# Rope of the up-projected queries: exchanging the halves by transfers in place of a second product

## The reference, cut to what matters

```python
def _rope(x, cos, sin):
    half = x.shape[-1] // 2
    x1, x2 = x[..., :half], x[..., half:]
    return jnp.concatenate([x1 * c - x2 * s, x2 * c + x1 * s], axis=-1)

def _mla(cq, ckv, kr, g_q, w_q_up, g_kv, w_kv_up, cos, sin):
    q = (_rms(cq, g_q) @ w_q_up).reshape(B, L, MLA_HEADS, MLA_NOPE + MLA_ROPE)   # 4 heads of 128 + 64, rank 256
    q_nope = q[..., :MLA_NOPE]
    q_rope = _rope(q[..., MLA_NOPE:], cos[:, None, :], sin[:, None, :])
```

## Time and profile before

| what | value |
|---|---|
| median of 3 runs | 2604.51 us |
| profiled execution, its own time | 2604.58 us |
| its span, first to last instruction | 2602.8 us |
| mean granted TensorE clock | 0.998 |
| TensorE (PE) busy | 2547.2 us, 98% |
| VectorE (DVE) busy | 1616.4 us, 62% |
| ScalarE (ACT) busy | 1213.5 us, 47% |
| GpSimd (POOL) busy | 334.6 us, 13% |

### The profile page before, as it was taken

One profiled execution on the slowest core, in us unless ns is written; L12 is line 12 of the kernel. 1 busy time (PEld: TensorE's weight loads), 2 busy tenths in 40 slices (PEclk: granted clock), 3 DMA queues, 4 the chain that ended last, 5 costly groups with the idle time before them and its releaser, 6 DMA issues.

```text
span 2602.8 us, 35370 instructions
## 1 busy us (share of the span) xinstructions
PE 2547.2 (98%) x12220; PEld 2106.9 (81%) x12220; DVE 1616.4 (62%) x3499; ACT 1213.5 (47%) x2183; POOL 334.6 (13%) x366
## 2 busy tenths in 40 slices
PE   8999999999999999999999999999999999999998
PEld 7998888676667888877877888888888888888886
DVE  6123306998995676664458677776757465564665
ACT  6112314777765555554545333533335353443554
POOL 2110002222221222210000000000000001111143
PEclk9999999999999999999999999999999999999999
DMA  6334458553332111135677767757655365666787
GB/s 232 121 106 125 126 163 253 143 135 85 95 131 90 35 32 38 36 111 162 195 244 217 227 197 237 222 177 222 192 155 181 107 225 110 168 168 159 202 165 138
DMA packets 329436, 398.59 MB, mean 153 GB/s; under 512 B 21408, under 2 KB 235664, under 8 KB 320944
## 3 DMA queue, kind: packets, MB, share of 16 engines
q1 hardware_dynamic: 311696, 364.41, 44.6%
q0 software_dynamic: 17568, 31.99, 8.0%
HBM read 239.86 MB, written 156.48 MB: 152 GB/s over the span
## 4 chain that ended last, share of the span: by engine, by line
PE 62%; DVE 3%; DMA 2%; ACT 1%; issue 1%; SPq 0%; POOL 0%; DVEq 0%; ACTq 0%; POOLq 0%
PE ff_ps_x L3248 26%; PE ff_ps_m L3248 13%; PE ff_ps_z L3248 6%; PE ml_ps_s L2125 6%; PE ff_ps_m L1685 4%; PE ml_ps_o L2154 4%; PE ml_ps_t L2138 2%; DMA ml_v_raw<-scr_yT 1%; DMA ff_pieces<-scr_acc 0%; PE ff_ps_r L2685 0%; PE mo_ps_t L2702 0%; SPq L2312 0%; DVE ff_pieces L2415 0%; DVE ff_pieces L2606 0%; DVE ff_pieces L2602 0%
## 5 line engine op out<-in xcount | busy, mean ns | idle before, releaser
L3248 PE MATMUL ff_ps_x<-ff_mv_hi_p,ff_st_hi_p 128*128 128x512 f32 x764 | 297.8, 390 | 0.5 <-ACT ff_u L2988 0.5
L3248 PE MATMUL ff_ps_x<-ff_mv_lo_p,ff_st_hi_p 128*128 128x512 f32 x764 | 297.3, 389 | 0.0
L3248 PE MATMUL ff_ps_x<-ff_mv_hi_p,ff_st_lo_p 128*128 128x512 f32 x764 | 297.3, 389 | 0.0
L2125 PE MATMUL ml_ps_s<-wide,ml_qs 128*128 128x416 f32 (+14 forms) x880 | 195.2, 354 | 4.0 <-PEq L137 2.7
L3094 DVE TENSOR_TENSOR ff_st_lo_p<-ff_ps_m,ff_st_hi_p 128x512 fp32r<-128x512 f32 x190 | 130.7, 688 | 103.4 <-ACT ff_st_hi_p L2971 103.4
L2938 POOL DMA_DIRECT2D scr_acc<-ff_pieces x64 | 55.6, 874 | 1015.2 <-DVE ff_pieces L3118 946.7
L2988 ACT ACTIVATE ff_u<-ff_ps_x 128x512 f32<-128x512 f32 x128 | 76.6, 598 | 215.0 <-PE ff_ps_x L3248 215.0
L3248 PEld LDWEIGHTS ff_ps_x<-ff_mv_hi_p,ff_st_hi_p 128*128 128x128 f32 x764 | 143.4, 188 | 32.5 <-issue 2.0
L3248 PEld LDWEIGHTS ff_ps_x<-ff_mv_hi_p,ff_st_lo_p 128*128 128x128 f32 x764 | 143.4, 188 | 29.9
L3248 PEld LDWEIGHTS ff_ps_x<-ff_mv_lo_p,ff_st_hi_p 128*128 128x128 f32 x764 | 143.4, 188 | 29.6
L2125 PEld LDWEIGHTS ml_ps_s<-wide,ml_qs 128*128 128x128 f32 x880 | 149.5, 188 | 20.0 <-issue 7.0
(11 more groups left out here) (316 smaller groups left out, 6380.4 us busy)
## 6 DMA issues: line engine op xcount, KB each, us to landing
st_raw<-in_w_ff SPq DMA_DIRECT2D x64, 512.0 KB, 6.2
scr_hid<-ff_pieces SPq DMA_DIRECT2D x128, 256.0 KB, 2.7
st_raw<-scr_hid SPq DMA_DIRECT2D x64, 512.0 KB, 5.4
ring<-in_w_ff SPq DMA_DIRECT2D x28, 1024.0 KB, 7.6
scr_t<-ring SPq DMA_DIRECT2D x24, 1024.0 KB, 5.8
ring<-scr_t SPq DMA_DIRECT2D x21, 1024.0 KB, 7.6
scr_acc<-ff_pieces POOLq DMA_DIRECT2D x64, 256.0 KB, 3.8
ring<-scr_u SPq DMA_DIRECT2D x13, 1024.0 KB, 8.2
```

The lines of the kernel that those rows point to most:

```text
L2125: m = pe.matmul(ps_s[n % NSB][:, 0:w], q, k, start=j == 0, stop=j == len(pairs) - 1)
L3248: m = pe.matmul(bank[:, :], w[kind][:, k], a[kind][:, k], start=start and k == 0 and i == 0, stop=stop and k == KH - 1 and i == 2, skip_gr ...
```

## The change: what it does

- A rope job makes one product (6 matmuls) in one bank. ACT copies it to one of four places (`rots`). SP exchanges the halves of each head by four transfers of 32 partitions, within SBUF (`swap`). VectorE multiplies the copy and the exchanged copy by cosines and sines in place (`finish`), POOL adds, SP stores.
- `FINISH_AT` says after which job the ropes of each piece are finished: those of piece 0 after rope (1, 1), of piece 1 after rope (2, 1), of piece 2 after rope (3, 1), of piece 3 after the last q job.
- The q jobs go behind the last rope. Takers of q and vo jobs are now ACT, ACT, VectorE in turn.
- The rope weights are split in the value pass, before ACT's last copy and after VectorE's last low part there; the exchanged weights and their four loads are gone.
- `UP_OUTS` is 6. The wait for all rope sums moves from the first transposes of the first head to its group 2.

```diff
@@ cv_proj, scalar
             for n in range(N):
                 m, rows = N + n, TILES[n][1]
+                if n == N - 1:
+                    act.wait_ge(up.gained, QR // P)
+                    act.activation(up.rope_hi[:, :, :], up.q_raw[:, :, NQF:WQ], ACT.Copy).then_inc(up.rope_hi_ready, 1)
@@ cv_proj, vector
             low(N - 1, pt[(N - 1) % 2])
+            dve.wait_ge(up.rope_hi_ready, 1)
+            dve.tensor_tensor(up.rope_lo[:, :, :], up.q_raw[:, :, NQF:WQ], f32(up.rope_hi[:, :, :]), ALU.subtract).then_inc(up.rope_lo_ready, 1)
@@
-WQ = NQF + 2 * NR
-UP_Q_LOADS = 4 * (QR // P) + 1
+WQ = NQF + NR
+UP_Q_LOADS = 2 * (QR // P) + 1
@@ mla_up, the jobs
-        jobs += [("q", 0, h) for h in range(MLA_H)] + [("turn", TURN_V)] + ropes_of(2) + folds_of((0, 1)) + ropes_of(3) + folds_of((2, 3))
-        WO_AT = {jobs.index(("rope", piece, 0)): piece - 2 for piece in (2, 3)}
+        jobs += [("turn", TURN_V)] + ropes_of(2) + folds_of((0, 1)) + ropes_of(3) + [("q", 0, h) for h in range(MLA_H)] + folds_of((2, 3))
+        WO_AT = {jobs.index(("turn", TURN_V)): 0, jobs.index(("rope", 3, 0)): 1}
+        FINISH_AT = {jobs.index(job): (2 * piece, 2 * piece + 1)
+                     for piece, job in enumerate((("rope", 1, 1), ("rope", 2, 1), ("rope", 3, 1), ("q", 0, MLA_H - 1)))}
@@
-            takers.append({"rope": "dve", "turn": "dve", "fold": "dve"}.get(kind) or ("act", "dve")[copies % 2])
+            takers.append({"rope": "act", "turn": "dve", "fold": "dve"}.get(kind) or ("act", "act", "dve")[copies % 3])
@@ sync
+            def swap(r):
+                sp.wait_ge(taken["act"], taken_by[ropes[r]])
+                raw, changed = (rots[r % ROTS][:, j] for j in range(2))
+                for p0 in range(0, P, ROPE):
+                    for to, of in ((0, ROPE // 2), (ROPE // 2, 0)):
+                        sp.dma_start(changed[p0 + to:p0 + to + ROPE // 2], raw[p0 + of:p0 + of + ROPE // 2]).then_inc(swapped[r % ROTS], 16)
+            for i, (kind, *args) in enumerate(jobs):
+                if kind == "rope":
+                    if args == [2, 0]:
+                        load_first_rest(sp, io, scr, ahead, 1)
+                    if args == [3, 0]:
+                        load_first_head(sp, io, scr, ahead, 2)
+                    swap(ropes.index(i))
+                elif i in stores:
+                    store(i)
+                for r in FINISH_AT.get(i, ()):
+                    store(ropes[r])
@@ gpsimd
-                pool.wait_ge(taken["dve"], taken_by[i])
+                pool.wait_ge(finished, r + 1)
@@ scalar
+                elif kind == "rope":
+                    r = ropes.index(i)
+                    if r >= ROTS:
+                        act.wait_ge(added, r - ROTS + 1)
+                    act.wait_ge(sums_ready, i + 1)
+                    act.activation(rots[r % ROTS][:, 0], at(i)[:, :], ACT.Copy).then_inc(taken["act"], 1)
@@ vector
+            def finish(r):
+                piece = jobs[ropes[r]][1]
+                dve.wait_ge(trig_loaded[piece], 16)
+                dve.wait_ge(swapped[r % ROTS], 64 * (r // ROTS + 1))
+                for part in range(2):
+                    m = dve.tensor_tensor(rots[r % ROTS][:, part], rots[r % ROTS][:, part], trig[:, part, cols(piece)], ALU.mult)
+                m.then_inc(finished, 1)
@@ vector, after each job
+                for r in FINISH_AT.get(i, ()):
+                    finish(r)
@@
-UP_OUTS = 8
+UP_OUTS = 6
```

More of the change, by code:

```diff
@@ L857, in mla_up @@
             first_banks.append(bank)
-            bank += 2 if kind == "rope" else 1
+            bank += 1
         ahead.up_taken = [(taken[who], takers[:-LAST].count(who)) for who in taken]
@@ L861, in mla_up @@
         ahead.ropes_added = added
-        stores = [i for i, job in enumerate(jobs) if job[0] in ("q", "vo", "rope")]
         ropes = [i for i, job in enumerate(jobs) if job[0] == "rope"]
+        stores = []
+        for i, job in enumerate(jobs):
+            stores += [i] * (job[0] in ("q", "vo")) + [ropes[r] for r in FINISH_AT.get(i, ())]
+        outs = {i: n for n, i in enumerate(stores)}
         folds = [i for i, job in enumerate(jobs) if job[0] in ("turn", "fold")]
@@ L881, in before @@
         def before(last):
-            return max((i for i, b in enumerate(first_banks) for w in range(2 if jobs[i][0] == "rope" else 1)
-                        if b + w <= last - NB), default=None)
+            return max((i for i, b in enumerate(first_banks) if b <= last - NB), default=None)
         def slot(engine, i):
@@ L908, in _, with store @@
                 sp.dma_start(ahead.lam[:, j], src.broadcast_to([P, DA_HD])).then_inc(ahead.lam_loaded, 16)
-            for i in stores:
+            def store(i):
                 kind, a, b = jobs[i]
-                if kind == "rope" and b == 0 and a >= 2:
-                    if a == 2:
-                        load_first_rest(sp, io, scr, ahead, 1)
-                    else:
-                        load_first_head(sp, io, scr, ahead, a - 1)
                 if kind == "rope":
@@ L997, in _ @@
                     pe.wait_ge(shared.v_copied, len(TILES))
-                last = before(first_banks[i] + (kind == "rope"))
+                last = before(first_banks[i])
                 for who in taken:
```

59 lines of the change are left out of this document (24 added, 35 removed).

## The result

The changed kernel takes 2624.18 us, the median of 4 runs (2622.29 to 2625.27); the kernel before took 2605.07 beside it, also the median of 4 (2604.35 to 2606.84). The medians are 19.1 us apart. The ratio is 1.0064, with a 95% interval of 1.0052 to 1.0076, which is 13.5 to 20 us: the change makes the kernel slower, well clear of noise. Forecast were 2612.0 and a range up to 2617. The direction and the two stalls came as foreseen; the price, by medians, was more than twice the forecast of 7.5 us.

A forecast was written before the change was run, and what follows sets the result against it. TensorE bounds the up-projection, VectorE nearly as much the attention after it. VectorE's later start +7.0, clock +1, given back -0.5 make +7.5 on 2604.5: 2612.0 us, range 2601 to 2617.

The forecast's parts named there:

- the two stalls: Up-projection: TensorE stands 13.4 us before its first vo product, then from near 434 to 440 after four score chunks.
- TensorE's saving: Rope jobs: 48 of 96 matmuls removed, 10.9 us, and the 1.68 us wait before the first rope product gone.
- the backlog: SP's queue: earlier loads hold exchange 0, issued by 403.9, so that it lands at about 413.4.
- Rivals 2 and 3: Rival 2: first exchanges not held by queued loads, 2604.6, chance 0.27; rival 3: exchanges cheap and fast, 2599, chance 0.11.
- The first stall: VectorE stands at its first finishes until exchange 0 lands at 413.4; TensorE stands still 13.4 us before vo.
- the second stall: SP's list and the last exchanges delay VectorE's attention start to 440.0 from 432.97, 7.0 us later.
- The wait for q 3's place: VectorE's last vo copy needs the output place of q 3, whose store lands at 439.4.
- The clock after the second stall: TensorE's products run at half speed for a few us, costing 0 to 2 us, taken as 1.
- given back: Attention, 432 to 440: VectorE's free time and ready first scores recover 0.5 us, between 0 and 1.5.
- The gain on offer: Up-projection: without any new wait TensorE reaches the attention 12.6 us sooner, at 419.5; 0.5% of the kernel.
- rival 3: SP's queue: exchanges cost 0.33 us each and land in 2 us; attention starts at 427.6, time 2599; chance 0.11.

The follow-up runs named there:

- Dve_adds: Changed kernel with the eight rope sums made by VectorE behind its multiplies instead of by POOL; ratio 1.0064, stage 52.6 us.
- Unread: Changed kernel with its 32 exchanges still issued from SP, but from a table into a place nobody reads; ratio 1.0040, stage 49.0 us.
- No_swap: Changed kernel without its 32 exchanges, VectorE multiplying the raw product by both tables; ratio 0.9995, stage 39.5 us.
- one_copy: Changed kernel with one 128-partition transfer per rope, halves not exchanged, in place of four of 32 partitions; ratio 1.0061, stage 51.8 us.
- no_swap_old: Changed kernel without its exchanges and with the order of jobs of the kernel before; ratio 1.0011, stage 39.2 us.
- early_split: Kernel before with only its rope weights (1024 columns) split in the value pass; ratio 0.9992, stage 38.7 us.
- split_back: Changed kernel with the rope weights split at the up-projection's start again; ratio 1.0070, stage 55.4 us.

## Why the prediction was wrong

**Right.** TensorE's saving (48 products; the first rope product right behind the transposes); the backlog (first multiply 413.86, forecast 413.4); the place and releaser of both stalls; that SP's list and the last exchanges set the end. In the backlog there is some luck: exchange 0 was issued at 401.13, 0.75 us before the forecast's 401.88, and still came 0.5 us later. Rivals 2 and 3 are refuted by the landings (the first four transfers 10.3 us after their issue, in the median) and by 0.63 us for each transfer. The first stall was 16.0 for 13.4 us: TensorE was dry at 404.4 and not 405.4, the landing was 0.5 late, and VectorE's two finishes took 3.5 us in place of 2.4. The fixed cost of 2.0 us that the prediction takes from the Trainium skill (DMA: Bandwidth & Descriptors, Anatomy of one DMA) is worked out there for transfers that GpSimd issues; here, on SP's queue, exchange 5 took 2.0 us in the median of its four and the other seven 3.1 to 10.3.

**The step that failed** is the sum of the second stall, "the attention at 440.0". Its mechanism was right, its terms were too small. In the order of the forecast:

| term | forecast | measured | more |
|---|---|---|---|
| rope 1's store issued | 417.75 | 421.1 | 3.4 |
| exchanges 4 to 7, issue | 8.0 | 10.0 | 2.0 |
| loads and stores between | 8.2 | 9.3 | 1.1 |
| SP through with exchange 7 | 433.95 | 440.49 | 6.5 |
| finishes 6 and 7 done | 437.7 | 445.75 | 8.1 |
| last copies, first attention instruction | 440.0 | 447.08 | 7.1 |

Nearly half of it comes in with the first term, and there with the POOL sum taken as 1.28 us: it took 3.25 (2.0 more), the multiplies ahead of it 2.35 for 1.2 (1.1 more), and the landing was 0.5 late. The next 3.1 us are SP's: 0.63 us for a transfer where 0.50 were taken, and slower loads and stores between. At the end VectorE gets exchange 6 at 442.26, 4.8 us behind its issue where 2 to 3 were forecast, and the last two finishes take 3.5 us for 1.7, again beside a sum. The row from which the price of a sum came, showed sums beside multiplies out of PSUM, and the change moved both operands into SBUF; the forecast read the instruction and not its operands' place. Dve_adds, which takes that contention away and puts the sums on VectorE's own list, won 3.0 us of the stage. The issue cost of 0.63 us was inside its bounds of 0.37 to 0.65, but 0.50 was read off stores of 128 partitions. The wait for q 3's place, forecast until 439.4, did not show, hidden behind the finishes. Unread, where VectorE waits 8.04 us for a place, shows that it stands right behind them.

**What came on top.** The clock after the second stall cost 1.9 us for a forecast of 1, inside its bounds; nothing was given back. 0.6 us came later, and 2.1 in the tail.

**The gain on offer** of 12.6 us was wrong as well, and hid behind the larger error. It took TensorE as the only bound of the stage if nothing waited. No_swap, with no exchange, keeps 1.0 us of it in the stage and nothing behind it. What takes its room there, by the rows, are the chains of ACT and VectorE through the splits of w_o, VectorE's finishes beside the sums, the places and the clock; they were not taken away one by one. So even free exchanges would not have given rival 3 its 5 us here. That rival has a slip besides: only 24 of the 32 transfers stand before what it sums, which is 4.1 us for its 5.4. And the sum writes the first stall as 12.9 us where the working has 13.4; neither changes the forecast.

**What stays open:** how the 9.5 us of unread divide between SP's issue time and the traffic of 2 MB; one_copy, which cut 24 issues and kept the bytes, won 3.7 us. Which of the old order's two waits in no_swap_old is due to the places and which to the shorter cover was read from rows, not tried. No kernel here beats the one before by more than its interval; early_split, at 0.9992, is the nearest.

## What to carry to other kernels

An engine that is 98% busy is a bound only as far as its work covers the others' chains: before halving its products in a stage, follow the longest chain of the other engines through it and ask what will cover that. Replacing a product by small transfers puts their issue into a queue that SP or ACT works in order (20 of the stage's 55 us here), and makes their landing hang on the loads in flight (10.3 us behind twelve loads, 3.1 later); price both, and the stores that come behind them. When an edit moves an operand from PSUM to SBUF, a duration read from the trace of before no longer holds beside GpSimd's work.

## What the runs showed of the hardware that was not expected

**A clock that falls by chance.** At the end of the differential attention TensorE waits 2.77 us in every kernel. In the trace of before the clock stays at 1.00 behind it; in that of one_copy it falls to 0.50. The rows are of before, then of one_copy, each with the first product behind the wait and the clock of a stretch some 4 us later:

```profile
784.00:788.00 4.00, 4.00 (x22) 2.57 (x21) 0.44 (x1) 2.13 (x4) 0.00 (x0) 1.00 0.83 222
...
780.01 1.48 PE L1632 MATMUL da_ps_t<-ident,da_rows 128*16 128x128 f32 x12 [2.78 <-DVE da_rows L1566]
```

```profile
796.00:800.00 4.00, 4.00 (x11) 2.21 (x11) 1.23 (x2) 0.60 (x1) 0.00 (x0) 0.50 0.74 204
...
792.83 1.89 PE L1661 MATMUL da_ps_t<-ident,da_rows 128*16 128x128 f32 x12 [2.77 <-DVE da_rows L1594]
```

From the first product with `da_v_meta` to the first with `ml_ps_s` it is 339.2 or 339.3 us in the traces of before, changed, split_back, no_swap and unread, where the clock stays, and 341.3 to 343.9 in the eleven others, where it falls for some microseconds. So the profiled executions of one_copy and dve_adds lost 3.2 and 4.0 us here that the changed kernel's did not, as much as their shorter stages had won; that is why the kernels are compared above by the stage's length. The same kernel's time moves with its clock: of the kernel before, 30 executions beside the experiments with a mean granted clock of 0.998 took 2602.8 to 2607.1 us, and 5 with 0.994 took 2610.7 to 2612.0. The Trainium skill (TensorE: Matmul & The Clock Gate, Part 1) has the chip watch windows that do not start with the kernel; that the same wait is followed by either level agrees with this, though no run here moved the wait alone.

**Small transfers.** Four transfers of 32 partitions from SBUF to SBUF cost 2.44 to 2.64 us of issue on SP and on ACT alike, but for a single issue of 1.0 to 1.5 us now and then; one of 128 partitions cost 0.52 to 0.68 us in seven cases and 1.46 in the eighth. The landings differ by a factor of three for the same 64 KB: 10.3 us behind the loads at 401, 3.1 us for exchange 7 at 438 to 440, the medians of four.
